# Modulation products of a transformer block: from two stationary columns and one accumulation to 32 stationary columns over four partition groups

## The chip, the cores and the metric

The program runs on one NeuronCore of one Trainium2 chip. The metric is the device time of one execution in microseconds (us). Before the change the median of three runs is 2926.92 us (2926.91 to 2927.85).

## What is computed

Two layers, one after the other, on 1024 tokens of width 1024. The part that the change touches is the modulation of the first layer: a conditioning vector `c` and a second one `c_ctx` go through silu and are multiplied with the 1024 x 6144 matrix `w_ada`; the six slices of the product shift, scale and gate the tokens.

```python
silu_c, silu_cc = silu(c), silu(c_ctx)[None]
mod_x = silu_c @ w_ada + b_ada                # 6 slices of 1024: sh1, sc1, g1, sh2, sc2, g2
mod_c = silu_cc @ w_ada + b_ada               # only the first two slices are used
hx = rms_norm(x, norm1_g) * (1 + sc1) + sh1   # needs slices 0 and 1
hc = rms_norm(ctx, norm1_g) * (1 + csc1) + csh1
qx, kx, vx, ux = split(hx @ w_in)             # keys and values of hc as well
attn = neighbourhood_attention(rope(qx), qx, rope(kx), vx, kc, vc, rpb)
conv = conformer_conv(ux, dw_kernel, ...)     # 31 taps
x = x + g1 * (concat(attn, conv) @ w_out)     # slice 2
x = x + g2 * squared_relu_mlp(rms_norm(x, norm2_g) * (1 + sc2) + sh2)   # slices 3, 4, 5
```

Behind it come the second layer (latent attention, a gated short convolution, attention over a memory) and a last norm, which the change leaves alone.

## The kernel before

Activations lie transposed: features on the 128 partitions, tokens in the free dimension. Weights come from memory in units of 128 x 1024 floats into `w_raw` (two buffers); GpSimd splits each into `w_hi` and `w_lo`, and TensorE makes each fp32 product of three faster products (L264 to L266). Each engine runs its own instruction list in the order in which the code writes it, and engines meet only on semaphores (`reach` waits for a count).

The first two slices of the modulation, 2048 columns, are made at the start, in four groups g of 512 columns (`ada_*`, L430 to L474). SP loads a group, 2048 KB, into one of two buffers; the loads of groups 2 and 3 wait until the products of groups 0 and 1 are done. TensorE takes silu of both vectors as the stationary operand, 2 columns for each of the 8 blocks of the contraction, and the group's columns as the moving one, and sums the 8 products in PSUM rows 0 and 1 (L449). ScalarE copies these two rows to `ada_row` (L464), TensorE turns them by four transposes so that the features come to lie on the partitions (L441), and VectorE adds the bias (L471 to L474). With that the first norm can be applied (`norm_act` L404, `norm_dve` L417 and L411), and with its first block the projections begin (L264).

The other four slices, 4096 columns, are made beside the neighbourhood attention (`late_*`, L488 to L521). The attention has 64 tiles (8 heads of 8 tiles of 128 queries). In step i TensorE makes the scores of tile i (L790 to L792), turns the probabilities of tile i-2 (L678), and makes the values of tile i-3 (L690). For odd tiles `late_pe` puts one late product in front of the values: the turn of the one before (L490) and then 8 products of 2 stationary columns with 128 moving ones (L500). Over the attention that is 32 late products, one for two tiles. Their weights use the two buffers of `w_raw`. VectorE in its step takes the row maximum with the bias (L742, L746), moves a part of the turned probabilities (L757), takes the late result (L505, L511) and scales the values (L765, L767), and then makes one or two taps of the convolution (L814). ScalarE takes the exponential (L711) and the other part of the move (L260). GpSimd makes the bias tables (L843).

One fp32 product, L449, L500, L678 or L690, may show as one or two records of TensorE in the profile: a transpose is one, an ordinary fp32 product is two.

The same code has `packed_sums` (L332 to L335): four products of 32 stationary columns each, into PSUM partitions 0, 32, 64 and 96. L910 in `ln_variance_pe` writes the same four groups, but four products in a row to the same group.

Of the kernel before, what the change touches and what calls it, by code (L numbers as in the profile page):

```python
# [23 lines left out]
ALU = mybir.AluOpType  # L24
ACT = mybir.ActivationFunctionType
AX = mybir.AxisListType.X

P = 128
T = 1024
TT = T // P  # L30
HALF = 512
D = 1024
KD = D // P
# [62 lines left out]
def build(nc, x_t, ctx_t, mem_t, w_ada, w_ada_late, units, small, rope_c, rope_s, rpb_pad, mask, positions, out, x_spill,  # L96
# [7 lines left out]
    def fixed(name, shape, offset, dt=F32):  # L104
        return nc.alloc_sbuf_tensor_at(name, [P, *shape], dt, offset=base + offset)

    def place(name, shape, kib, dt=F32):

        return nc.alloc_sbuf_tensor_at(name, [P, *shape], dt, offset=arena + int(kib * 1024))

    KIB = 1024
    w_raw = fixed("w_raw", [2, 1024], 0)
# [3 lines left out]
    ident = fixed("ident", [P], 40 * KIB)  # L116
    ones = fixed("ones", [P], 40 * KIB + 512)
    par = fixed("par", [N_SMALL], 41 * KIB)
    der = fixed("der", [N_DERIVED], 41 * KIB + (4 * N_SMALL + 31) // 32 * 32)
    assert 4 * N_SMALL + 32 + 4 * N_DERIVED <= 2 * KIB  # L120

    def sp_(name, n=1, k=0):
        return par[:, SMALL[name] + k:SMALL[name] + k + n]
# [1 line left out]

    mod_x, mod_c = der[:, 0:48], der[:, 48:64]
    a1, a1c, a2 = der[:, 64:72], der[:, 72:80], der[:, 80:88]
    silu_c = der[:, 88:104]
    qh_s, mq_s = der[:, 104:105], der[:, 105:106]
    one_col = der[:, 106:107]  # L130
    eps_col = der[:, 107:108]
    both_g = der[:, 128:136]
    row_max, neg_max, row_sum, inv_sum = (der[:, 112 + 4 * i:116 + 4 * i] for i in range(4))


    ada_buf = place("ada_buf", [2, KD, HALF], 0)
    ada_row = place("ada_row", [2, HALF], 32)
    ctx_sb = place("ctx_sb", [KD, CTX], 36)
# [23 lines left out]
    late_row = place("late_row", [P], 62)  # L162
# [47 lines left out]
    region = nc.alloc_psum_tensor("region", [P, 2, T], F32)  # L210
    aux = nc.alloc_psum_tensor("aux", [P, T], F32)
    pv = nc.alloc_psum_tensor("pv", [P, 2, HALF], F32)
# [5 lines left out]
    def sem(name):  # L218

        tag, _, what = name.partition("_")  # L220
        if tag in SHARED:
            name = f"{SHARED[tag][0]}_{what}"
        if name not in sems:
            sems[name] = nc.alloc_semaphore(name)
        return sems[name]

    def reach(e, name, value):

        tag, _, what = name.partition("_")
        if tag in SHARED:  # L230
            kind, before = SHARED[tag]
            value = value + sum(COUNTS.get(f"{t}_{what}", n) for t, n in before)
        e.wait_ge(sem(name), value)

    raw_loaded = [sem("raw_loaded_0"), sem("raw_loaded_1")]
    free = [sem("region_free_0"), sem("region_free_1")]
# [17 lines left out]
    def wait_region(e, use):  # L254

        if use >= 2:
            e.wait_ge(free[use % 2], use // 2)

    def copy(e, dst, src, **kw):
        return e.activation(dst, src, ACT.Copy, **kw)  # L260
# [169 lines left out]
    def ada_sp(e, pos):  # L430
        for g in range(N_ADA):
            if g >= 2:
                reach(e, "ada_mm", g - 1)
            e.dma_start(ada_buf[:, g % 2], w_ada[g]).then_inc(sem(f"ada_ld{g % 2}"), 16)

    def ada_pe(e, pos):
        def turn(g):
            reach(e, "ada_row", g + 1)
            for j in range(4):
                m = 4 * g + j  # L440
                last = e.transpose(pv[:, 0, 2 * m:2 * m + 2], ada_row[0:2, g % 2, j * P:(j + 1) * P], ident[0:2, 0:2])  # L441
            last.then_inc(sem("ada_tr"), 1)

        for g in range(N_ADA):
            use = pos.next_use()
            wait_region(e, use)
            reach(e, f"ada_ld{g % 2}", 16 * (g // 2 + 1))
            for k in range(KD):
                last = e.matmul(region[0:2, use % 2, 0:HALF], silu_c[:, 2 * k:2 * k + 2], ada_buf[:, g % 2, k],  # L449
                                start=(k == 0), stop=(k == KD - 1))  # L450
            last.then_inc(sem("ada_mm"), 1)
            if g:
                turn(g - 1)
        turn(N_ADA - 1)

    def ada_act(e, pos, ch):
        for g in range(N_ADA):
            use = pos.next_use()
            reach(e, "ada_mm", g + 1)
            if g >= 2:  # L460
                reach(e, "ada_tr", g - 1)
            copy(e, ada_row[0:2, g % 2], region[0:2, use % 2, 0:HALF]).then_inc(free[use % 2], 1)
            e.wait_ge(free[use % 2], use // 2 + 1)
            e.sem_inc(sem("ada_row"), 1)  # L464

# [10 lines left out]
    def constants_dve(e, ch):  # L476
        ch(e.memset(eps_col, EPS))
        e.sem_inc(sem("eps"), 1)
        reach(e, "small_ld", 16)
        ch(e.tensor_scalar(qh_s, sp_("qh"), QK ** -0.5, None, ALU.mult))  # L480
        ch(e.tensor_tensor(both_g, sp_("final", 8), sp_("norm_2", 8), ALU.mult))
        ch(e.tensor_scalar(mq_s, sp_("mq"), P ** -0.5, None, ALU.mult))
# [4 lines left out]
    N_LATE = 32  # L487

    def late_turn(e):
        return e.transpose(pv[:, 1, 256:258], late_row[0:2], ident[0:2, 0:2])  # L490

    def late_pe(e, i):
        if i % 2 == 0:
            return
        n = i // 2
        if n:
            late_turn(e)
        reach(e, f"late_ld{n % 2}", 16 * (n // 2 + 1))
        for k in range(KD):
            last = e.matmul(pv[0:2, 1, P:2 * P], silu_c[:, 2 * k:2 * k + 2], w_raw[:, n % 2, k * P:(k + 1) * P],  # L500
                            start=(k == 0), stop=(k == KD - 1))
        last.then_inc(sem("late_used"), 1)

    def late_add(e, ch, n):
        ch(e.tensor_tensor(mod_x[:, 16 + n:17 + n], pv[:, 1, 256:257], sp_("b_ada", 1, 16 + n), ALU.add))  # L505

    def late_dve(e, ch, i):
        if i % 2:
            if i > 1:
                late_add(e, ch, i // 2 - 1)  # L510
            ch(e.tensor_copy(late_row[0:2], pv[0:2, 1, P:2 * P]))  # L511

    def late_end_pe(e, pos):
        reach(e, "na_stored", HEADS * TT)
        late_turn(e).then_inc(sem("late_tr"), 1)
# [1094 lines left out]
    with nc.Block() as block:  # L1610
        @block.sync
        def _(sp):
            def load(u, s):
                sp.dma_start(w_raw[:, s], units[u]).then_inc(raw_loaded[s], 16)

            sp.dma_start(par[:], small).then_inc(sem("small_ld"), 16)
            ada_sp(sp, None)
            load(0, 0)
            load(1, 1)

            def load_range(a, b):
                with sp.Fori(a // 2, b // 2) as i:
                    for s in range(2):

                        sp.wait_ge(unit_split, i * 2 + (s - 1))
                        sp.dma_start(w_raw[:, s], units[i * 2 + s]).then_inc(raw_loaded[s], 16)

            load_range(2, ATTN_SPLIT)
            for s in range(2):
                sp.wait_ge(unit_split, ATTN_SPLIT - 1 + s)  # L1630
                sp.dma_start(w_raw[:, s], w_ada_late[s]).then_inc(sem(f"late_ld{s}"), 16)
            with sp.Fori(1, N_LATE // 2) as i:
                for s in range(2):

                    reach(sp, "late_used", i * 2 + (s - 1))
                    sp.dma_start(w_raw[:, s], w_ada_late[i * 2 + s]).then_inc(sem(f"late_ld{s}"), 16)
            reach(sp, "late_used", N_LATE)
            load_range(ATTN_SPLIT, N_UNITS)
            for j in range(KD):
                reach(sp, "out_ready", j + 1)  # L1640
                sp.dma_start(out[:, j], x3[:, j]).then_inc(sem("out_st"), 16)
            reach(sp, "out_st", 16 * KD)
# [42 lines left out]
        def _(act):  # L1685
            pos = Pos()
            ch = Chain(act, "scalar_step")
# [3 lines left out]
            act.dma_start(sin1[:], rope_s).then_inc(sem("rope1_ld"), 16)  # L1691
            act.dma_start(cos1[:], rope_c).then_inc(sem("rope1_ld"), 16)
            reach(act, "small_ld", 16)
            act.activation(silu_c, sp_("c", 16), ACT.Silu).then_inc(sem("silu_c"), 1)
            reach(act, "eps", 1)
            rms_act(act, ch, "r1", lambda k: x_sb[:, k], KD, T, D,
                    scale_from_ready=lambda k: reach(act, f"x_ld{k // 4}", 16))
            ada_act(act, pos, ch)
            reach(act, "ctx_ld", 16)
            norm_act(act, ch, "n1", KD, T, h_hi, lambda k: a1[:, k:k + 1], lambda k: mod_x[:, k:k + 1])  # L1700
# [59 lines left out]
        def _(dve):  # L1760
            pos = Pos()
            ch = Chain(dve, "vector_step")
            constants_dve(dve, ch)
            rms_dve(dve, ch, "r1", T)
            ada_dve(dve, pos, ch)
# [52 lines left out]
        def _(pe):  # L1818
# [11 lines left out]
            rms_pe(pe, "r1", KD, T)  # L1830
            reach(pe, "silu_c", 1)
            ada_pe(pe, pos)
            proj1_pe(pe, pos)
            tell()
# [194 lines left out]
```

## Time and profile before

| what | value |
|---|---|
| timed runs | 2926.92 us median of 3 |
| span of the profiled execution | 2924.9 us, 2.0 us under that median; the page gives no other time of that execution |
| TensorE busy | 2797.3 us, 96% |
| VectorE, ScalarE, GpSimd busy | 1366.1 us, 701.2 us, 937.5 us |
| modulation at the start (L449, L441) | 27.7 to 58.2 us |
| attention with the late products | 338.6 to 686.4 us |

The span runs from the first to the last instruction. The records of matmuls are pipelined: a record starts when its weights go in or its columns begin to stream, and the next may start before it ends.

### The profile page before, as it was taken

To read this page: it belongs to the slowest core of one execution; us is meant where nothing else is said; L and a number is where in the kernel's file an instruction comes from. 1 tells how busy PE (TensorE), PEld (TensorE's weight loads), DVE (VectorE), ACT (ScalarE), POOL (GpSimd) and SP (SyncE) were. 2 spreads that over 40 slices of the span, in tenths; PEclk is the share of its full clock that TensorE was granted. 3 is DMA by queue.
4 is the path that set the end of the run, shared out by engine and by line. 5 is a ranking of instruction groups with operands and counts; after the bars stand their busy time and mean duration, and the time that the engine had idled before them with its cause. 6 is when DMAs were issued, how large, how long until landed. Compare 5 with 4: busy or idle time off the path is not lost.

```text
span 2924.9 us, 34818 instructions
## 1 busy us (share of the span) xinstructions
PE 2797.3 (96%) x14040; PEld 2262.7 (77%) x14040; DVE 1366.1 (47%) x1493; ACT 701.2 (24%) x972; POOL 937.5 (32%) x443
## 2 busy tenths in 40 slices
PE   7999799998989999999988989999999999999899
PEld 2888577775868888888876769998888878878777
DVE  2735877774354454444457666663102231251331
ACT  3300133333131122121114445442100020141010
POOL 1334422110434353444432310002433434433333
PEclk9999799999989999999999999999999999999999
DMA  5111222112101111111111100000111111112112
GB/s 232 37 37 52 75 67 62 59 50 90 51 29 51 43 51 50 50 50 43 50 65 72 38 21 1 1 1 30 45 64 51 50 36 51 58 51 101 43 36 87
DMA packets 36673, 155.88 MB, mean 53 GB/s; under 512 B 4164, under 2 KB 4296, under 8 KB 35016
## 3 DMA queue, kind: packets, MB, share of 16 engines
q1 hardware_dynamic: 33264, 127.04, 13.0%
q10 hardware_dynamic: 1528, 20.71, 1.8%
q0 software_dynamic: 1760, 6.36, 0.9%
q8 instruction: 94, 1.54, 0.2%
q14 instruction: 27, 0.22, 0.0%
HBM read 145.70 MB, written 8.39 MB: 53 GB/s over the span
## 4 chain that ended last, share of the span: by engine, by line
PE 88%; DVE 8%; ACT 2%; DMA 1%; issue 1%; POOL 1%; DVEq 0%; ACTq 0%; POOLq 0%
PE region L264 21%; PE region L265 21%; PE region L266 21%; PE pv L690 8%; PE aux L678 4%; DVE conv L814 3%; PE region L790 2%; PE pv L500 2%; PE pv L341 1%; PE region L792 1%; PE aux L350 1%; PE region L449 1%; DVE tmp L417 1%; DVE h_lo L411 1%; DMA rs_again<-rs_spill 1%
## 5 line engine op out<-in xcount | busy, mean ns | idle before, releaser
L1649 POOL TENSOR_TENSOR w_hi<-w_raw,der 128x1024 fp32r<-128x1024 f32 x186 | 359.3, 1932 | 1713.5 <-PE region L266 1661.8
L264 PE MATMUL region<-h_hi,w_hi 128*128 128x512 f32 x1760 | 694.8, 395 | 40.8 <-DVE h_lo L411 17.8
L265 PE MATMUL region<-h_lo,w_hi 128*128 128x512 f32 x1760 | 690.6, 392 | 0.0
L266 PE MATMUL region<-h_hi,w_lo 128*128 128x512 f32 x1760 | 690.1, 392 | 0.0
L1652 POOL TENSOR_TENSOR w_lo<-w_raw,w_hi 128x1024 fp32r<-128x1024 f32 x186 | 497.2, 2673 | 14.6
L264 PEld LDWEIGHTS region<-h_hi,w_hi 128*128 128x128 f32 x1760 | 333.8, 190 | 119.9 <-issue 45.6
L266 PEld LDWEIGHTS region<-h_hi,w_lo 128*128 128x128 f32 x1760 | 333.8, 190 | 70.5
L265 PEld LDWEIGHTS region<-h_lo,w_hi 128*128 128x128 f32 x1760 | 334.0, 190 | 68.4
L264 PE MATMUL region<-ff_hi,w_hi 128*128 128x512 f32 x512 | 199.2, 389 | 0.0
L265 PE MATMUL region<-ff_lo,w_hi 128*128 128x512 f32 x512 | 199.2, 389 | 0.0
L266 PE MATMUL region<-ff_hi,w_lo 128*128 128x512 f32 x512 | 199.2, 389 | 0.0
L814 DVE SCALAR_TENSOR_TENSOR conv<-glu,par,conv 128x1024 f32<-128x1024 f32 x120 | 187.2, 1560 | 2.1
L1038 DVE TENSOR_TENSOR tmp<-tmp 128x1024 f32<-128x1024 f32 x32 | 63.8, 1995 | 184.5 <-ACT tmp L1010 184.5
L843 POOL TENSOR_TENSOR bias_t<-toep,mask_t 128x640 f32<-128x640 f32 x40 | 64.3, 1610 | 217.3 <-DVE der L746 217.2
L1052 DVE TENSOR_TENSOR tmp<-tmp 128x1024 f32<-128x1024 f32 x56 | 115.3, 2097 | 35.6 <-ACT tmp L1021 35.6
L690 PE MATMUL pv<-v,prob_t 128*128 128x128 f32 x1024 | 124.6, 275 | 0.0
L690 PEld LDWEIGHTS pv<-v,prob_t 128*128 128x128 f32 x1024 | 119.3, 192 | 0.0
L749 DVE TENSOR_REDUCE der<-region 128x1 f32<-128x1024 f32 (+1 forms) x96 | 91.5, 954 | 56.9 <-PE region L266 52.0
L1044 DVE SCALAR_TENSOR_TENSOR x<-region,der,x 128x1024 f32<-128x1024 f32 x32 | 41.1, 1283 | 152.7 <-PE region L266 152.7
L264 PEld LDWEIGHTS region<-ff_hi,w_hi 128*128 128x128 f32 x512 | 96.1, 188 | 20.0
L266 PEld LDWEIGHTS region<-ff_hi,w_lo 128*128 128x128 f32 x512 | 96.1, 188 | 19.9
L265 PEld LDWEIGHTS region<-ff_lo,w_hi 128*128 128x128 f32 x512 | 96.1, 188 | 19.9
(316 smaller groups left out, 4164.0 us busy)
## 6 DMA issues: line engine op xcount, KB each, us to landing
w_raw<-units SPq DMA_DIRECT2D x186, 512.0 KB, 3.6
w_raw<-w_ada_late SPq DMA_DIRECT2D x32, 512.0 KB, 3.7
ada_buf<-w_ada SPq DMA_DIRECT2D x4, 2048.0 KB, 11.9
toep<-rpb_pad POOLq DMA_DIRECT2D x16, 288.0 KB, 5.0
x_sb<-x_t ACTq DMA_DIRECT2D x2, 2048.0 KB, 13.6
x<-x_t ACTq DMA_DIRECT2D x1, 4096.0 KB, 14.3
x_spill<-x ACTq DMA_DIRECT2D x1, 4096.0 KB, 11.8
x<-x_spill ACTq DMA_DIRECT2D x1, 4096.0 KB, 14.4
```

The lines of the kernel that those rows point to most:

```text
L264: pe.matmul(dst, wh, xh, start=first, stop=False)
L265: pe.matmul(dst, wh, xl, start=False, stop=False)
L266: return pe.matmul(dst, wl, xh, start=False, stop=last)
L678: last = e.transpose(aux[:, b * P:(b + 1) * P], self.prob[:, i % 2, b * P:(b + 1) * P], ident[:])
L690: last = e.matmul(pv[:, i % 2, 0:P], self.prob_t[:, i % 2, b], self.v_of(i, b), start=(b == 0), stop=(b == self.nkt - 1))
L749: e.tensor_reduce(neg_max[:, i % 4:i % 4 + 1], region[:, use % 2, 0:self.nkeys], AX, ALU.max, negate=True).then_inc(self.s("maxed"), 1)
L814: ch(e.scalar_tensor_tensor(out=conv[:, j], in0=src, scalar=w, in1=conv[:, j], op0=ALU.mult, op1=ALU.add))
L843: e.tensor_tensor(bias_t[:, v, 0:KEYS].rearrange("p (r c) -> p r c", c=W_GRID), toep[h % 2][:, r0:r0 + 10], mask_t[:, v].rearrange("p (r c ...
L1038: e.tensor_tensor(tmp[:, 2 + f % 2], tmp[:, f % 2], tmp[:, f % 2], ALU.mult).then_inc(sem("ff_sq"), 1)
L1052: e.tensor_tensor(tmp[:, 2 + i], tmp[:, 2 + i], tmp[:, i], ALU.add).then_inc(sem("nf_acc"), 1)
L1649: pool.tensor_tensor(w_hi[:, s], w_raw[:, s], one_col.broadcast_to([P, 1024]), ALU.mult)\
L1652: pool.tensor_tensor(w_lo[:, s], w_raw[:, s], w_hi[:, s].bitcast(F32), ALU.subtract)\
```

## The change

The stationary operand of each block is widened from 2 to 32 columns (the two silu vectors repeated 16 times, `silu_wide`). Block k of the contraction goes to PSUM partitions 32 (k mod 4) to 32 (k mod 4) + 31, so that each group of partitions sums two blocks only. The four partial sums are added by the turn: instead of a transpose of two rows it is an ordinary fp32 product of the whole 128-row result with `quad`, 128 x 2, which has a one in column c for rows c, c+32, c+64 and c+96. The copies take 128 rows instead of 2. The semaphores `ada_mm` and `late_used` are raised by the last product of each group, so four times. VectorE makes `quad` once. To make room in SBUF, the scratch memory for DMA descriptors gets 8192 bytes a partition, which the program did not set before.

```diff
-            act.activation(silu_c, sp_("c", 16), ACT.Silu).then_inc(sem("silu_c"), 1)
+            act.activation(silu_wide[:].rearrange("p k (n two) -> p k n two", two=2),
+                           sp_("c", 16).rearrange("p (k two) -> p k two", two=2).unsqueeze(2).broadcast_to([P, KD, 16, 2]),
+                           ACT.Silu).then_inc(sem("silu_c"), 1)
...
             for j in range(4):
                 m = 4 * g + j
-                last = e.transpose(pv[:, 0, 2 * m:2 * m + 2], ada_row[0:2, g % 2, j * P:(j + 1) * P], ident[0:2, 0:2])
+                last = e.matmul(pv[:, 0, 2 * m:2 * m + 2], ada_row[:, g % 2, j * P:(j + 1) * P], quad, start=True, stop=True)
...
             for k in range(KD):
-                last = e.matmul(region[0:2, use % 2, 0:HALF], silu_c[:, 2 * k:2 * k + 2], ada_buf[:, g % 2, k],
-                                start=(k == 0), stop=(k == KD - 1))
-            last.then_inc(sem("ada_mm"), 1)
+                quarter = slice(32 * (k % 4), 32 * (k % 4) + 32)
+                last = e.matmul(region[quarter, use % 2, 0:HALF], silu_wide[:, k], ada_buf[:, g % 2, k], start=(k < 4), stop=(k >= 4))
+                if k >= 4:
+                    last.then_inc(sem("ada_mm"), 1)
...
-            copy(e, ada_row[0:2, g % 2], region[0:2, use % 2, 0:HALF]).then_inc(free[use % 2], 1)
+            copy(e, ada_row[:, g % 2], region[:, use % 2, 0:HALF]).then_inc(free[use % 2], 1)
...
+        reach(e, "consts", 4)
+        e.tensor_reduce(quad, ident[:].rearrange("p (q c) -> p c q", c=32)[:, 0:2], AX, ALU.add).then_inc(sem("quad"), 1)
...
-        return e.transpose(pv[:, 1, 256:258], late_row[0:2], ident[0:2, 0:2])
+        return e.matmul(pv[:, 1, 256:258], late_row[:], quad, start=True, stop=True)
...
         for k in range(KD):
-            last = e.matmul(pv[0:2, 1, P:2 * P], silu_c[:, 2 * k:2 * k + 2], w_raw[:, n % 2, k * P:(k + 1) * P],
-                            start=(k == 0), stop=(k == KD - 1))
-        last.then_inc(sem("late_used"), 1)
+            quarter = slice(32 * (k % 4), 32 * (k % 4) + 32)
+            last = e.matmul(pv[quarter, 1, P:2 * P], silu_wide[:, k], w_raw[:, n % 2, k * P:(k + 1) * P], start=(k < 4), stop=(k >= 4))
+            if k >= 4:
+                last.then_inc(sem("late_used"), 1)
...
-    nc = _bacc.Bacc("TRN2", target_bir_lowering=False, num_devices=1)
+    nc = _bacc.Bacc("TRN2", target_bir_lowering=False, num_devices=1, dynamic_dma_scratch_size=8192)
```

No instruction changes its place; what changes is what stands there. TensorE at the start, groups 0 to 2 of the early modulation, before (`region` is the PSUM tile, `der` held silu and `ident` the identity):

```order
L449 MATMUL region<-ada_buf,der 2x512 [waits ada_ld0,silu_c]
L449 MATMUL region<-ada_buf,der 2x512 x7
L449 MATMUL region<-ada_buf,der 2x512 [waits ada_ld1]
L449 MATMUL region<-ada_buf,der 2x512 x7
L441 MATMUL pv<-ident,ada_row 128x2 [waits ada_row]
L441 MATMUL pv<-ident,ada_row 128x2 x3
L449 MATMUL region<-ada_buf,der 2x512 [waits ada_ld0,region_free_0]
L449 MATMUL region<-ada_buf,der 2x512 x7
```

and the same place now (`der` here is `quad`):

```order
L452 MATMUL region<-ada_buf,silu_wide 32x512 [waits ada_ld0,silu_c]
L452 MATMUL region<-ada_buf,silu_wide 32x512 x7
L452 MATMUL region<-ada_buf,silu_wide 32x512 [waits ada_ld1]
L452 MATMUL region<-ada_buf,silu_wide 32x512 x7
L443 MATMUL pv<-der,ada_row 128x2 [waits quad,ada_row]
L443 MATMUL pv<-der,ada_row 128x2 x3
L452 MATMUL region<-ada_buf,silu_wide 32x512 [waits ada_ld0,region_free_0]
L452 MATMUL region<-ada_buf,silu_wide 32x512 x7
```

The products have 32 rows of output in place of 2, and the turn waits for `quad` too.

TensorE in the attention, one step with a late product, before:

```order
L792 MATMUL region<-k_ctx,q_t 128x256
L678 MATMUL aux<-ident,na_prob 128x128 [waits att_pt_b,att_pt_a,att_prob]
L678 MATMUL aux<-ident,na_prob 128x128 x6
L490 MATMUL pv<-ident,late_row 128x2 [waits att_stored,att_pt_b,att_pt_a]
L500 MATMUL pv<-w_raw,der 2x128 [waits late_ld1]
L500 MATMUL pv<-w_raw,der 2x128 x7
L690 MATMUL pv<-v_tok,na_prob_t 128x128 x5
L690 MATMUL pv<-v_ctx,na_prob_t 128x128 x2
```

and now (the lines have moved by five to six):

```order
L798 MATMUL region<-k_ctx,q_t 128x256
L684 MATMUL aux<-ident,na_prob 128x128 [waits att_pt_b,att_pt_a,att_prob]
L684 MATMUL aux<-ident,na_prob 128x128 x6
L495 MATMUL pv<-der,late_row 128x2 [waits att_stored,att_pt_b,att_pt_a]
L506 MATMUL pv<-w_raw,silu_wide 32x128 [waits late_ld1]
L506 MATMUL pv<-w_raw,silu_wide 32x128 x7
L696 MATMUL pv<-v_tok,na_prob_t 128x128 x5
L696 MATMUL pv<-v_ctx,na_prob_t 128x128 x2
```

The waits are the same, and the number of products is the same.

## Rows read from the trace of the kernel before

**Rows 1.** Page, part 4: the chain that ended last, by engine.

```profile
PE 88%; DVE 8%; ACT 2%; DMA 1%; issue 1%; POOL 1%; DVEq 0%; ACTq 0%; POOLq 0%
```

**Rows 2.** Chain of waits, 26 to 66 us: start us, us, what.

```profile
27.75 6.97 PE region L449 x16
...
34.74 7.85 DMA ada_buf<-w_ada
...
42.73 7.03 PE region L449 x16
...
50.09 6.97 PE region L449 x16
...
57.08 0.60 ACT ada_row L260
...
57.77 0.42 PE pv L441 x4
...
58.28 0.18 DVE der L471
```

**Rows 3.** Timeline at 420 to 434 us: start us, us, instruction, [idle before <- releaser].

```profile
421.72 1.92 DVE L814 SCALAR_TENSOR_TENSOR conv<-glu,par,conv 128x1024 f32<-128x1024 f32 x1
...
422.36 0.98 PE L678 MATMUL aux<-ident,na_prob 128*128 128x128 f32 x7
...
423.28 0.22 PE L490 MATMUL pv<-ident,late_row 2*128 2x2 f32 x1
...
423.43 1.91 PE L500 MATMUL pv<-w_raw,der 128*2 128x128 f32 x16
...
425.26 1.38 PE L690 MATMUL pv<-v_tok,na_prob_t 128*128 128x128 f32 x10
...
428.73 0.98 PE L678 MATMUL aux<-ident,na_prob 128*128 128x128 f32 x7
...
429.55 1.28 PE L690 MATMUL pv<-v_tok,na_prob_t 128*128 128x128 f32 x10
```

**Rows 4.** Timeline at 1532 us, the packed sums, two calls in a row.

```profile
1532.86 0.20 PEld L334 LDWEIGHTS aux<-tmp,ones 128*32 128x32 f32 x8 [7.09 <-DVE tmp L1052]
1532.87 1.94 PE L334 MATMUL aux<-tmp,ones 128*32 128x256 f32 x16 [6.67 <-DVE tmp L1052]
1533.30 0.20 PEld L334 LDWEIGHTS aux<-tmp,ones 128*32 128x32 f32 x4 [0.23 <-issue]
```

**Rows 5.** Timeline at 1642 us: packed sums, then unpacked products.

```profile
1642.01 0.64 PE L334 MATMUL aux<-tmp,ones 96*32 96x256 f32 x8
1642.58 1.99 PE L341 MATMUL pv<-head_scale,ident 128*128 128x256 f32 x8
```

**Rows 6.** Chain of waits over the whole span, at the layer norm.

```profile
709.36 5.71 PE aux L910 x28
```

**Rows 7.** Groups by line, 350 to 686 us: busy us, mean ns, idle before.

```profile
L814 DVE SCALAR_TENSOR_TENSOR conv<-glu,par,conv 128x1024 f32<-128x1024 f32 x75 | 108.7, 1449 | 0.6
...
L742 DVE CUSTOM_DVE_ANT_0 na_prob<-region,bias_t 128x896 f32<-128x896 f32 x62 | 67.7, 1091 | 26.4 <-PE aux L678 23.4 <-DVE conv L814 2.0
...
L500 PE MATMUL pv<-w_raw,der 128*2 128x128 f32 x512 | 61.1, 272 | 0.0
...
L505 DVE TENSOR_TENSOR der<-pv,par 128x1 f32<-128x1 f32 x31 | 4.9, 158 | 46.8 <-PE pv L690 46.8
```

**Rows 8.** Busy time by stretch: PE, PEld, DVE, ACT, POOL, clock, DMA share, GB/s.

```profile
4.00:8.00 4.00, 0.00 (x0) 0.00 (x0) 0.47 (x3) 0.91 (x2) 0.00 (x0) 1.00 1.02 429
64.00:68.00 4.00, 3.11 (x7) 2.48 (x8) 3.93 (x4) 3.60 (x4) 0.00 (x0) 0.50 0.00 0
```

**Rows 9.** Timeline of GpSimd at 51 us and of GpSimd and VectorE at 336 us.

```profile
51.00 1.89 POOL L1649 TENSOR_TENSOR w_hi<-w_raw,der 128x1024 fp32r<-128x1024 f32 x1 [49.34 <-DMA w_raw<-units]
...
336.34 2.29 POOL L843 TENSOR_TENSOR bias_t<-toep,mask_t 128x640 f32<-128x640 f32 x1
...
342.21 1.09 DVE L742 CUSTOM_DVE_ANT_0 na_prob<-region,bias_t 128x896 f32<-128x896 f32 x1 [3.71 <-PE region L792]
```

More of the change, by code:

```diff
@@ L127, in build @@
     a1, a1c, a2 = der[:, 64:72], der[:, 72:80], der[:, 80:88]
-    silu_c = der[:, 88:104]
     qh_s, mq_s = der[:, 104:105], der[:, 105:106]
@@ L132, in build @@
     both_g = der[:, 128:136]
+    quad = der[:, 136:138]
     row_max, neg_max, row_sum, inv_sum = (der[:, 112 + 4 * i:116 + 4 * i] for i in range(4))
+    silu_wide = place("silu_wide", [KD, 32], 164)
     ada_buf = place("ada_buf", [2, KD, HALF], 0)
@@ L432, in ada_sp @@
             if g >= 2:
-                reach(e, "ada_mm", g - 1)
+                reach(e, "ada_mm", 4 * (g - 1))
             e.dma_start(ada_buf[:, g % 2], w_ada[g]).then_inc(sem(f"ada_ld{g % 2}"), 16)
@@ L438, in turn @@
             reach(e, "ada_row", g + 1)
+            reach(e, "quad", 1)
             for j in range(4):
                 m = 4 * g + j
-                last = e.transpose(pv[:, 0, 2 * m:2 * m + 2], ada_row[0:2, g % 2, j * P:(j + 1) * P], ident[0:2, 0:2])
+                last = e.matmul(pv[:, 0, 2 * m:2 * m + 2], ada_row[:, g % 2, j * P:(j + 1) * P], quad, start=True, stop=True)
             last.then_inc(sem("ada_tr"), 1)
@@ L458, in ada_act @@
             use = pos.next_use()
-            reach(e, "ada_mm", g + 1)
+            reach(e, "ada_mm", 4 * (g + 1))
             if g >= 2:
                 reach(e, "ada_tr", g - 1)
-            copy(e, ada_row[0:2, g % 2], region[0:2, use % 2, 0:HALF]).then_inc(free[use % 2], 1)
+            copy(e, ada_row[:, g % 2], region[:, use % 2, 0:HALF]).then_inc(free[use % 2], 1)
             e.wait_ge(free[use % 2], use // 2 + 1)
@@ L510, in late_dve @@
                 late_add(e, ch, i // 2 - 1)
-            ch(e.tensor_copy(late_row[0:2], pv[0:2, 1, P:2 * P]))
+            ch(e.tensor_copy(late_row[:], pv[:, 1, P:2 * P]))
     def late_end_pe(e, pos):
@@ L1633, in _ @@
                 for s in range(2):
-                    reach(sp, "late_used", i * 2 + (s - 1))
+                    reach(sp, "late_used", i * 8 + 4 * (s - 1))
                     sp.dma_start(w_raw[:, s], w_ada_late[i * 2 + s]).then_inc(sem(f"late_ld{s}"), 16)
-            reach(sp, "late_used", N_LATE)
+            reach(sp, "late_used", 4 * N_LATE)
             load_range(ATTN_SPLIT, N_UNITS)
```

## The prediction

> **What bounds the kernel now.** I read the chain that ended last first: TensorE holds 88% of it [rows 1], so work taken from TensorE shortens the run wherever nothing else is close behind. Then the two places the change touches. At the start the chain goes through the 16 records of L449 of group 0, the load of group 2 that waited for them (7.85 us), the records of group 2 and of group 3, the copy, the turn, and the addition on VectorE at 58.28 [rows 2]. The reader is to see that the loads of groups 2 and 3 start only when the products of groups 0 and 1 are done, and that everything of layer one waits for 58.28. In the attention I read one step from the timeline: 0.22 us of turn (L490), then 16 records of L500 from 423.43, and the values (L690) at 425.26, with no idle time of TensorE [rows 3]. So the late product is on the path, 1.84 us of it with the drain behind it, 32 times. Last, the groups by line: VectorE still has idle time there, 46.8 us in front of L505 and 26.4 us in front of L742 [rows 7].
>
> **The late product.** Nothing here shows 32 stationary columns with 128 moving fp32 columns in four partition groups. The nearest row is the packed sums: 8 fp32 products in a row to groups 0, 1, 2, 3, 0, 1, 2, 3, which is the order of the new code. They show 16 records, and their weight loads lie in bunches, 8 at 1532.86 and the next 4 at 1533.30 [rows 4]: four products run at a time, and a wave of 256 columns takes 0.43 us there. The 16 records take 1.94 us in all; at 0.43 a record one after the other they would take 6.9. At the other clock level the same call of 8 records takes 0.64 us, against 1.99 us for 8 unpacked records of the same width [rows 5]. Taking the end of a record off (a 256-column record lasts 0.38 beyond the last start, as 1.99 less 7 spacings of 0.23), a wave costs 0.24 against 8 spacings of about 0.23.
>
> Before, 16 records of L500 take 1.84 us up to the next line, 0.109 us each ((1.91 - 0.27) / 15, with 0.272 for the length of one record [rows 3, 7]) and 0.09 of drain behind the last. After, they are four waves. The first needs its weights, 0.03 us; then three spacings of 0.109 and 0.02 for the stagger of four give the last start at 0.38; L690 comes 0.08 before the last record's end as before [rows 3], so with 0.27 - 0.08 behind it, L690 begins 0.57 us after the block's start. That is 1.27 us saved a time.
>
> The turn becomes an ordinary fp32 product with 128 rows, so two records of 128 weights each, 0.11 us apart as in L690 [rows 3], where a transpose was one. But L490 starts only 0.06 us before L678 ends, while L690 behind L678 in the step without a late product starts 0.16 us before it [rows 3]: the two-row transpose pays 0.09 for a change of the array's shape, and the 128-row turn doesn't. So +0.11 - 0.09, with a little less tail; I take it as -0.03, between -0.05 and +0.11 us a time. Sum in the attention: 32 x (1.27 + 0.03) = 41.6 us. Bounds: 32 x (1.27 - 0.11) = 37 and 43; the unpacked bound, no overlap at all, is a rival below.
>
> The Trainium skill, "TensorEngine Tiling (Array Packing)", Key Properties, says that changing the tiling mode drains TensorE. By that rule packing would add two drains to each late step; the trace agrees that such a change costs (the 0.09 above), but shows it on both sides of L500 before the change, since 2 columns are already handled as a narrow tile. The rule with nothing paid before would put the sum 32 x 0.18 = 6 us higher; the rows say zero.
>
> **What hides beside it.** The copies L511 and L464 take 128 rows instead of 2, but the same 128 or 512 elements a row; I take the same time. The wider silu writes 256 elements a row instead of 16 before the first square is due; `quad` is one small reduction on VectorE, some 25 us before it is needed. Both cost nothing while the loads of x last. The late loads of 512 KB have a period of 9.25 us instead of 10.55 and two buffers, so they stay hidden. Four increments instead of one reach only SP, which is not waited for.
>
> The Trainium skill, "TensorE: Matmul & The Clock Gate", The cost: per-tile semaphore tail, gives about 26 ns for each increment of packed products. No run here shows several. By its figure, an estimate, three more in each of 32 blocks would be 2.5 us if TensorE waited for them.
>
> **The start.** Groups 0 and 1 are ready in SBUF when TensorE comes to them at 27.7. Records of 512 columns follow each other every 0.43 us (6.97 / 16) [rows 2]. Four waves instead of 16 records: group 0's last product starts at 27.7 + 0.03 + 3 x 0.43 + 0.02 = 29.0 and ends at 29.6, and the load of group 2 goes out there instead of at 34.74. It lands 7.85 us later, at 37.5. The load of group 3 goes out at 31.4 behind it in the queue; 2 MB at the 429 GB/s that the DMA engines reach at the start [rows 8] are 4.9 us, so it lands at 42.4. Now the loads bind, and what is faster on TensorE is only the tail: four waves, copy 0.60, turn. TensorE has been idle from 32 to 37.5 and again before 42.4; between 58.2 and 64.9 before it fell to the lower clock, 0.50 of the granted clock [rows 8], so I take group 3 at 1.2 GHz: four waves of 0.85 and 0.35 of fill and tail, 3.8; copy 0.7 with its semaphores; 8 records of the turn at 0.17 (between 0.11 at the full clock and 0.22 at half) and its end, 1.6. VectorE's addition comes at 42.4 + 6.1 = 48.5 to 48.8 instead of 58.28. At 2.4 GHz it would be 2.2 us earlier. GpSimd's split of the first unit starts when it lands: before at 51.00 [rows 9]; its load now goes out right behind group 3 and lands 1 to 2 us after it, near 45, its first pass is 1.89 us, both I put at 4 to 5, so it is done by 50. The first projection came at 64.9 (3.11 us busy up to 68) [rows 8], 6.6 us behind the addition; it is due at 55.3 and finds the unit split. Saved: 9.5 us, between 6 (the loads run at 350 GB/s, or share more) and 12 (full clock).
>
> **Sum.** 41.6 + 9.5 = 51.1 us. The profiled execution's span of 2924.9 becomes 2873.8; the timed median lies 2.0 us over the span, which gives 2875.8, rounded 2876. With both terms at their bounds: 2872 to 2884. Everything behind the attention keeps its length, within some 3 us for where the clock's lower stretches fall.
>
> **Rivals.**
>
> *VectorE takes over the attention.* It has 73 us of idle time over 32 pairs of steps, 2.3 us each [rows 7]; TensorE gives up 1.3, so VectorE needs 8.25 of the new 9.25 us on average. But the taps are uneven: 75 in 31 pairs, so four pairs in ten have three; and a tap takes 1.45 us on average [rows 7] and 1.92 beside GpSimd [rows 3]. A pair with three taps at 1.92 needs 8.25 - 2.4 x 1.45 + 5.76 = 10.5. If VectorE's lag reached TensorE, 13 such pairs would cost 16 us at most; with half of the taps slow, 8: 2884. Against it: TensorE asks in step i for what VectorE began a step earlier, so a lag of up to 2 us is made up in the next pair. It decides when VectorE's lag passes 2 us.
>
> *The groups overlap only in part.* L910, which sends four products in a row to one partition group, takes 5.71 us for 28 records, 0.20 each, no better than unpacked [rows 6]: the order of the groups matters. If the two halves of each product had to follow in order, a block of 8 products would be 9 slots instead of 4: 1.1 us, 23 us saved in the attention and some 4 at the start, 2900. Against it: L334 has the new code's order and shows four waves [rows 4].
>
> *Slower: each change of partition group drains the array.* Rows 3 price a change of shape at 0.09 us. Were that paid at each of the 7 changes of group in a block, without overlap, a late product would take 1.84 + 0.63, and the turn's second record 0.11 more: +24 us in the attention, +2 at the start, 2953. It decides if one change of group costs more than what overlaps. Rows 4 and 5 speak against it. Its mild form is that the change does nothing: no overlap, no drain, 2931 with the turn.
>
> *The smaller descriptor memory holds GpSimd up.* Four loads go out before the first bias table at 336.34; VectorE then waits 3.7 us for TensorE at 342.21 anyway [rows 9]. If the loads had to wait for each other, some 14 us late, 10 would show: 2886. Later in the attention GpSimd has time enough.
>
> **Chances.** Forecast 75% (with the increments of the skill in it, 2878). VectorE 10%, partial overlap 7%, descriptor memory 4%, slower 2%, nothing gained 2%. The range of 2866 to 2888 holds the forecast, most of VectorE's case and the descriptor memory's; below the forecast it leaves room for a full clock at the start and a better placed clock later. A change of 0.2% (6 us) is what a measurement of this kernel can tell from none: faster by more 0.96, within it 0.01, slower 0.03.
>
> **What would show it.** In the profile after: the records of the late product in four bunches, about 0.64 us in all, and the values 0.57 us after its start; steps with a late product 1.3 us shorter, and the idle time of VectorE before L505's successor down from 1.5 us to a few tenths; the attention some 41 us shorter. At the start: groups 0 and 1 done by 31.4, two waits of TensorE for `ada_buf`, the addition near 48.6 and the first projection near 55. Wrong would be: TensorE waiting in the attention for L757 or L742's buffers; weight loads in the block one after the other; a load of group 3 landing after 46; or other stages that change by more than 3 us.

## The result and the profile after

The changed kernel takes 2876.95 us (median of 4 runs, 2874.46 to 2878.76) against 2926.93 before: ratio 0.9831, 95% interval 0.9817 to 0.9845. 2876 was predicted. Its profiled execution spans 2875.7 us, 49.2 less than before.

The attention, first the chip's view of one late step, the lines that answer to [rows 3] (timeline of TensorE at 407 to 409 us):

```profile
407.01 0.98 PE L684 MATMUL aux<-ident,na_prob 128*128 128x128 f32 x7
407.83 0.28 PE L495 MATMUL pv<-der,late_row 128*128 128x2 f32 x2
408.04 0.64 PE L506 MATMUL pv<-w_raw,silu_wide 128*32 128x128 f32 x16
408.62 0.60 PE L696 MATMUL pv<-v_tok,na_prob_t 128*128 128x128 f32 x3
```

The 16 records of the late product take 0.64 us instead of 1.91, and the values begin 0.58 us after the block's start instead of 1.83. The turn has two records now, but begins 0.16 us before L684 ends, not 0.06, and they start only 0.03 us apart: from the start of L684 to the start of the product 1.03 us pass, 1.07 before. The groups by line at 341 to 638 us (busy, mean ns, idle before) answer to [rows 7]:

```profile
L820 DVE SCALAR_TENSOR_TENSOR conv<-glu,par,conv 128x1024 f32<-128x1024 f32 x76 | 113.3, 1490 | 0.6
...
L748 DVE CUSTOM_DVE_ANT_0 na_prob<-region,bias_t 128x896 f32<-128x896 f32 x62 | 67.7, 1092 | 19.9 <-PE aux L684 17.1 <-DVE conv L820 1.1
...
L511 DVE TENSOR_TENSOR der<-pv,par 128x1 f32<-128x1 f32 x32 | 5.0, 156 | 11.9 <-PE pv L696 11.3 <-PE pv L495 0.5
```

In front of the last two VectorE waits 31.8 us instead of 73.2; nearly all of what TensorE gave up came out of VectorE's idle time.

The start, in the chain of waits at 26 to 57 us (start us, us, what), answering to [rows 2]:

```profile
28.64 3.69 PE region L452 x32
...
32.34 11.05 DMA ada_buf<-w_ada
...
43.53 1.92 PE region L452 x16
45.45 1.89 PE pv L443 x16
...
47.43 0.19 DVE der L474
...
47.85 1.24 DVE der L476
49.09 0.02 issue
49.11 1.83 DVE der L477
50.94 0.02 issue
50.96 4.52 DVE tmp L418 x2
```

Both first groups take 3.69 us where one took 6.97. Then the loads bind, as forecast. TensorE's granted clock was 0.56 of full when group 2 was multiplied and 1.00 for group 3 (busy time by stretch, columns as in [rows 8]):

```profile
38.00:42.00 4.00, 3.38 (x17) 0.79 (x17) 0.00 (x0) 0.00 (x0) 0.00 (x0) 0.56 1.03 442
43.00:48.00 5.00, 3.80 (x32) 2.36 (x32) 0.50 (x3) 0.60 (x1) 3.18 (x2) 1.00 0.41 164
```

What follows the addition is longer now, 9.3 us to the first projection instead of 6.6. GpSimd's splits of the first two weight units ran from 51.00 to 59.58 before, so that only the last of them met VectorE's work, which began at 58.28. These are the lines of before (timeline):

```profile
57.24 2.34 POOL L1652 TENSOR_TENSOR w_lo<-w_raw,w_hi 128x1024 fp32r<-128x1024 f32 x1
...
58.70 0.90 DVE L473 SCALAR_TENSOR_TENSOR der<-der,par 128x8 f32<-128x8 f32 x1
```

Now three of the four passes lie beside VectorE (timelines of GpSimd and of VectorE, answering to [rows 9]):

```profile
44.74 1.89 POOL L1655 TENSOR_TENSOR w_hi<-w_raw,der 128x1024 fp32r<-128x1024 f32 x1 [43.08 <-DMA w_raw<-units]
...
46.72 2.34 POOL L1658 TENSOR_TENSOR w_lo<-w_raw,w_hi 128x1024 fp32r<-128x1024 f32 x1
49.01 1.89 POOL L1655 TENSOR_TENSOR w_hi<-w_raw,der 128x1024 fp32r<-128x1024 f32 x1
50.98 3.41 POOL L1658 TENSOR_TENSOR w_lo<-w_raw,w_hi 128x1024 fp32r<-128x1024 f32 x1
```

```profile
47.43 0.17 DVE L474 TENSOR_TENSOR der<-pv,par 128x16 f32<-128x16 f32 x1 [10.98 <-PE pv L443]
...
47.85 1.22 DVE L476 SCALAR_TENSOR_TENSOR der<-der,par 128x8 f32<-128x8 f32 x1
49.11 1.82 DVE L477 SCALAR_TENSOR_TENSOR der<-der,par 128x8 f32<-128x8 f32 x1
50.96 4.52 DVE L418 TENSOR_TENSOR tmp<-x_sb,tmp 128x1024 f32<-128x1024 f32 x2
```

The two operations on 8 columns, L476 and L477, take 1.22 and 1.82 us and the two norm products (L418) 4.52, against 0.17, 0.17 and 2.36 when nothing runs on GpSimd (see units first below). Compare the ends: GpSimd's passes end at 49.06 and 50.91, and L476 and L477 end 0.02 us behind each; before, L473 ended 0.02 us behind GpSimd's 59.58. The other way round it looks the same: L418's first product began at 50.96, 0.02 us ahead of GpSimd's last pass, which then took 3.41 us instead of 2.34. So the one that starts later waits until the other is done; it is not that both run more slowly. The addition L474, which reads PSUM, took its 0.17 us in the middle of a pass.

Where the time went, from the start of the same instruction in each profiled execution (first projection, first score, first product of the layer norm's mean; the timed median is of each kernel's own runs):

| kernel | first projection | first score | layer norm | attention | span | timed median | ratio to before, 95% |
|---|---|---|---|---|---|---|---|
| before | 64.9 | 338.6 | 687.2 | 348.6 | 2924.9 | 2926.9 | |
| after | 56.8 | 331.9 | 638.4 | 306.5 | 2875.7 | 2877.0 | 0.9831 [0.9817, 0.9845] |
| late only | 64.9 | 338.5 | 646.2 | 307.6 | 2881.3 | 2884.2 | 0.9861 [0.9844, 0.9877] |
| start only | 55.9 | 329.7 | 678.3 | 348.6 | 2919.5 | 2921.5 | 0.9989 [0.9979, 0.9998] |
| groups in pairs | 57.9 | 332.8 | 640.0 | 307.1 | 2873.4 | 2878.1 | 0.9839 [0.9823, 0.9856] |
| wide, one group | 58.6 | 332.3 | 682.0 | 349.7 | 2922.9 | 2923.8 | 0.9993 [0.9983, 1.0003] |
| two groups | 56.4 | 330.2 | 671.9 | 341.6 | 2907.0 | 2910.0 | 0.9945 [0.9925, 0.9965] |
| eight increments | 56.0 | 329.8 | 637.0 | 307.2 | 2874.4 | 2875.8 | 0.9828 [0.9808, 0.9848] |
| descriptor memory only | 64.9 | 339.8 | 688.4 | 348.7 | 2923.4 | 2926.6 | 1.0001 [0.9991, 1.0010] |
| more on VectorE | 56.2 | 331.2 | 657.0 | 325.8 | 2891.9 | 2894.7 | 0.9897 [0.9882, 0.9913] |
| units first | 52.5 | 326.3 | 633.9 | 307.6 | 2869.0 | 2871.6 | 0.9818 [0.9805, 0.9832] |
| four buffers | 53.2 | 326.9 | 634.5 | 307.6 | 2869.6 | 2872.5 | 0.9818 [0.9805, 0.9832] |
| four buffers, units third | 52.8 | 326.5 | 633.9 | 307.4 | 2870.6 | 2872.5 | 0.9815 [0.9799, 0.9831] |
| four buffers, units fourth | 55.3 | 330.3 | 636.8 | 306.5 | 2873.5 | 2872.4 | 0.9814 [0.9800, 0.9827] |

The kernel before was run again beside each; its medians were 2925.6 to 2926.9, and the ratios are to the runs beside.

The first projection is a noisy number. Seven kernels of the table have the start of the change unaltered (after, start only, groups in pairs, wide, two groups, eight increments, more on VectorE), and it comes at 55.9 to 58.6 us. In five of them group 3 is multiplied at the full clock, in 1.9 us; in the other two, groups in pairs and wide, the clock had not risen or had fallen again, and the same records take 3.6 and 3.3 us. These two have the latest first projections, 57.9 and 58.6.

### The profile page after: what moved, and what is told of

It is laid out like the page before. It is cut to its first block, busy times and chain, and to the rows that moved or that the text cites. A ratio compares the mean times of both kernels' runs of the same rounds, so it can differ in the third digit from the quotient of the medians.

```text
span 2875.7 us, 34919 instructions
## 1 busy us (share of the span) xinstructions
PE 2737.6 (95%) x14088; PEld 2236.7 (78%) x14088; DVE 1374.4 (48%) x1494; ACT 701.9 (24%) x972; POOL 939.2 (33%) x443
## 4 chain that ended last, share of the span: by engine, by line
PE 87%; DVE 8%; DMA 1%; ACT 1%; issue 1%; POOL 1%; DVEq 0%; ACTq 0%; POOLq 0%; SPq 0%
PE region L265 22%; PE region L267 21%; PE region L266 21%; PE pv L696 8%; PE aux L684 4%; DVE conv L820 3%; PE region L796 2%; PE pv L342 1%; PE region L798 1%; DVE tmp L418 1%; PE aux L351 1%; PE pv L506 1%; DVE h_lo L412 1%; DMA rs_again<-rs_spill 1%; DVE x L1597 1%
## 5 line engine op out<-in xcount | busy, mean ns | idle before, releaser
L1058 DVE TENSOR_TENSOR tmp<-tmp 128x1024 f32<-128x1024 f32 x56 | 115.2, 2096 | 35.6 <-ACT tmp L1027 35.6
L1050 DVE SCALAR_TENSOR_TENSOR x<-region,der,x 128x1024 f32<-128x1024 f32 x32 | 41.1, 1284 | 152.7 <-PE region L267 152.7
```

Source lines behind the costliest of these rows:

```text
L1058: e.tensor_tensor(tmp[:, 2 + i], tmp[:, 2 + i], tmp[:, i], ALU.add).then_inc(sem("nf_acc"), 1)
```

## Experiments

**Late products only.** The early ones as before (2 columns, transposes).

```diff
-                last = e.matmul(region[quarter, use % 2, 0:HALF], silu_wide[:, k], ada_buf[:, g % 2, k], ...)
+                last = e.matmul(region[0:2, use % 2, 0:HALF], silu_wide[:, k, 0:2], ada_buf[:, g % 2, k], ...)
```

> Only the late products of the attention are packed; the early ones are as before (2 stationary columns, one group, transposed turn). Theory (each late step gives 1.3 us, 42 us over the attention, and the start gives the rest): 2926.9 - 42.5 = 2884.5 us, first projection at 65 us as before, attention 306.5 us long (348.6 before). Rival (the attention was shortened by something else, such as the smaller descriptor memory or the shift in time): over 2890, or a step that isn't 1.3 us shorter.

Measured 2884.19 us; first projection unchanged at 64.9, attention 307.6 us, 41.0 shorter. The late products alone carry five sixths of the gain.

**Start only.** The late products as before.

```diff
-            last = e.matmul(pv[quarter, 1, P:2 * P], silu_wide[:, k], w_raw[...], start=(k < 4), stop=(k >= 4))
+            last = e.matmul(pv[0:2, 1, P:2 * P], silu_wide[:, k, 0:2], w_raw[...], start=(k == 0), stop=(k == KD - 1))
```

> Only the early products are packed; the late ones are as before. Theory: the first projection comes at 56.8 us instead of 64.9, of these 8.1 us 1.4 are given back on VectorE before the attention, so 2926.9 - 6.7 = 2920.2 us. By the prediction's own term (9.5 us) it would be 2917.4. The two single parts should add up to the whole change (42.5 + 6.7 = 49.2, measured 50).

Measured 2921.54 us. The start gives 9.0 us at the first projection and all of it still at the layer norm (678.3), but the span is only 5.4 shorter. The loss is in the MLP. At three places in it, where a group of columns begins (995, 1171 and 1348 us), TensorE waits for nothing that the profile shows, in the first as follows (timeline):

```profile
993.11 0.39 PE L267 MATMUL region<-h_hi,w_lo 128*128 128x512 f32 x1
995.07 0.39 PE L265 MATMUL region<-h_hi,w_hi 128*128 128x512 f32 x1 [1.57 <-issue]
```

The three cost 5.9 us together against the kernel before, and TensorE's clock, at the lower level for 3.4 us from 1348.8, another 1.6. The wide, unpacked kernel below has the same three waits and one such stretch, 8.6 us in all; the changed kernel has none of them. In either run 3 to 4 us come back by 2725 us, which was not followed up. TensorE's instructions not being there in time would look like this, but no run here isolates it, and the cause stays open. So the parts, 41.4 and 4.1 us of timed median, don't add up to 50, though their pieces at the start and in the attention do.

**Groups in pairs.** Does the order of the partition groups make the overlap?

```diff
-        for k in range(KD):
+        for k in (0, 4, 1, 5, 2, 6, 3, 7):
```

> The change, with the late products in the order of partition groups 0, 0, 1, 1, 2, 2, 3, 3. Theory (the order of the groups makes the overlap, as in L910 before): the two halves and the two products of a group follow each other, neighbours overlap only at the seams: 13 slots of 0.109 us instead of 4, 1.55 us a block, 32 x 0.98 = 31 us more, 2908 us. With 9 slots it would be 2894. Rival (TensorE looks far enough ahead to mix the groups by itself): four waves, 2877.

Measured 2878.12 us, attention 307.1. The theory that the order 0, 0, 1, 1 spoils the overlap falls: the timeline shows four waves as before.

```profile
409.05 0.67 PE L506 MATMUL pv<-w_raw,silu_wide 128*32 128x128 f32 x16
409.64 1.38 PE L696 MATMUL pv<-v_tok,na_prob_t 128*128 128x128 f32 x10
```

**Two groups.** Four products in a row to one group, then four to the next. The turn takes 64 rows instead of 128.

```diff
-            quarter = slice(32 * (k % 4), 32 * (k % 4) + 32)
+            half = slice(32 * (k // 4), 32 * (k // 4) + 32)
```

> The change, with the late products in two partition groups only, blocks 0 to 3 in group 0 and 4 to 7 in group 1, four products (8 records) in a row each; the turn takes 64 rows. The run with the groups in pairs showed that TensorE mixes the groups by itself when 4 records of one group stand in a row. Theory (it looks only a few records ahead, and L910 before, with 8 records of a group in a row, hardly overlaps): a block takes 1.4 to 1.8 us, 27 to 39 us more than the change, 2904 to 2916. Rival (it looks over all 16 records): 8 waves, 1.0 us, 14 us more, 2891.

Measured 2910.01 us, attention 341.6 us. The values begin 1.46 us after the block's start:

```profile
423.83 0.38 PE L495 MATMUL pv<-der,late_row 64*128 64x2 f32 x2
424.14 1.53 PE L506 MATMUL pv<-w_raw,silu_wide 128*32 128x128 f32 x16
425.60 1.38 PE L696 MATMUL pv<-v_tok,na_prob_t 128*128 128x128 f32 x10
```

The starts of single records in this block are 424.14, .28, .39, .50, .60 for group 0, and the first of group 1 comes at 424.61, when 3 of group 0's 8 are still to start. (A record does not name its group; the spacing of 0.11 us within a group and the semaphore's increments tell them apart.) With 4 records to a group in a row all four groups started within 0.04 us. This would fit a limit on how many records of one group may wait, about three, before TensorE takes in no more. L910 before [rows 6] fits it too: its single records start one by one and then in pairs 0.006 to 0.03 us apart. The limit is inferred from these orders, not shown. The block accounts for 28 of the 35 us by which this attention is longer than the changed kernel's; most of the rest is the turn. From the start of L684 to the start of the product 1.22 us pass here and 1.03 there, 6 us over 32 steps: a turn of 64 rows costs 0.19 us more than one of 128.

**Wide, one group.** 32 stationary columns, all blocks in group 0, turned by the transpose.

```diff
-            last = e.matmul(pv[quarter, 1, P:2 * P], silu_wide[:, k], w_raw[...], start=(k < 4), stop=(k >= 4))
+            last = e.matmul(pv[0:32, 1, P:2 * P], silu_wide[:, k], w_raw[...], start=(k == 0), stop=(k == KD - 1))
```

> The start as in the change; the late products with 32 stationary columns, but all in partition group 0, and turned by the transpose as before. Theory (widening costs and gives nothing, packing is all): a block stays 1.84 us, 2920 us as with the start alone. Rival (weights of 32 columns are in the way): 0.025 us for each of 16 x 32 records, 13 us more, 2933. Rival (widening itself helps): under 2915.

Measured 2923.78 us. The block is 1.93 us long, as with 2 columns, and the attention 349.7:

```profile
417.37 0.22 PE L495 MATMUL pv<-ident,late_row 2*128 2x2 f32 x1
417.52 1.93 PE L505 MATMUL pv<-w_raw,silu_wide 128*32 128x128 f32 x16
```

Widening costs 1.1 us in 32 blocks and gives nothing; the overlap of the groups is all. Against the run of the start alone the span is 3.4 us longer: 2.7 of it stand at the first projection, with group 3 at the lower clock, and 1.1 in the attention. What both are slower than 2920 lies in the waits of the MLP named above and, here, in the start.

**Eight increments.**

```diff
-            if k >= 4:
-                last.then_inc(sem("late_used"), 1)
+            last.then_inc(sem("late_used"), 1)
```

> The change, with an increment of the semaphore behind each of the 8 late products instead of the last four. Theory (TensorE doesn't wait for them): the values begin 0.57 us after the block's start, 2877 us. Rival (the Trainium skill, TensorE: Matmul & The Clock Gate, The cost: per-tile semaphore tail, gives about 26 ns for each increment): 0.10 us more a block, 3 us over the attention, 2880.

Measured 2875.79 us. The values begin 0.57 us after the block's start, as with four increments, so TensorE doesn't wait for them:

```profile
406.56 0.65 PE L506 MATMUL pv<-w_raw,silu_wide 128*32 128x128 f32 x16
407.13 1.38 PE L695 MATMUL pv<-v_tok,na_prob_t 128*128 128x128 f32 x10
```

**Descriptor memory only.** The kernel before with `dynamic_dma_scratch_size=8192`.

> The kernel before, with the smaller memory for DMA descriptors alone. Theory (it costs nothing): 2926 us, GpSimd's four loads before the first bias table go out 0.6 to 0.9 us apart as before. Rival (the loads wait for each other): up to 10 us more, 2936.

Measured 2926.6 us, ratio 1.0001, 95% interval 0.9991 to 1.0010: no cost that can be measured.

**More on VectorE.** How far off is the next bound?

```diff
             ch(e.tensor_copy(late_row[:], pv[:, 1, P:2 * P]))
+            ch(e.tensor_reduce(spare[:], glu[:, 0, 0:T], AX, ALU.max))
```

> The change, with one reduction of 1024 columns more on VectorE in each of the 32 late steps (about 1.1 us; its result isn't used). VectorE has some 30 us of idle time left in the attention, 0.95 a pair. Theory (VectorE is now close behind TensorE): the 1.1 us use up the idle time and 0.2 to 0.5 us a pair show: 5 to 15 us more, 2882 to 2892. Rival (its lag is absorbed, TensorE is the only bound): within 2 us of 2877. Rival (VectorE is already the bound): 32 x 1.1 = 35 us more, 2912.

Measured 2894.65 us; attention 325.8 us, 19.3 longer. Groups by line of VectorE, and below them TensorE's wait in the same stretch:

```profile
L750 DVE CUSTOM_DVE_ANT_0 na_prob<-region,bias_t 128x896 f32<-128x896 f32 x62 | 67.7, 1091 | 4.6 <-PE aux L686 1.9 <-DVE conv L822 0.8
L519 DVE TENSOR_REDUCE spare<-glu 128x1 f32<-128x1024 f32 x32 | 39.0, 1220 | 1.1
```

```profile
PE aux L686 <- DVE na_prob_t L765: 14.1, 18, 1.2
```

The reduction takes 1.22 us, 39.0 in all. About half of it was absorbed. Of the 19.3 us that show, TensorE waits 14.1 for VectorE (L765); some 3 more are two stretches of 3.4 us at the lower clock, from 498.1 and from 607.3, which the changed kernel doesn't have there. The theory was right in kind and too small in size: VectorE still has about 22 us of idle time left in this attention, so not all of it can be used. Why not was not tested; I think that the waits of one step lie where the next one can't reach them.

**The start: units first.** The loads of the first two weight units ahead of groups 2 and 3.

```diff
         for g in range(N_ADA):
+            if g == 2:
+                load(0, 0)
+                load(1, 1)
             if g >= 2:
```

> The change, with the first two weight units loaded ahead of groups 2 and 3 of the early modulation. In the change GpSimd splits them from 44.7 to 54.4 us, beside VectorE's additions and first norm, and three of VectorE's instructions there take 1.2 to 2.3 us instead of 0.2 to 1.2. Theory (that overlap costs the 2.6 us between the addition and the first projection, 9.3 against 6.7 before): the split moves to 27 to 37 us, beside the reciprocal, the first projection comes 2.6 us earlier, at 54.2, 2874 us. Rival (the loads are moved into the way of group 3, nothing gained): groups 2 and 3 unchanged at best, 2877; if they take the queue up to 2.5 us longer, 2877 to 2879.

Measured 2871.63 us (2870.74 to 2875.01), first projection at 52.5. The timeline of GpSimd and of VectorE:

```profile
34.24 2.34 POOL L1659 TENSOR_TENSOR w_lo<-w_raw,w_hi 128x1024 fp32r<-128x1024 f32 x1
```

```profile
47.08 0.17 DVE L479 SCALAR_TENSOR_TENSOR der<-der,par 128x8 f32<-128x8 f32 x1
47.28 0.17 DVE L480 SCALAR_TENSOR_TENSOR der<-der,par 128x8 f32<-128x8 f32 x1
47.48 2.36 DVE L418 TENSOR_TENSOR tmp<-x_sb,tmp 128x1024 f32<-128x1024 f32 x2
```

With GpSimd done at 36.6, the operations on 8 columns take 0.17 us again and the pair of norm products 2.36. From the addition to the first projection 5.9 us pass, 9.3 in the changed kernel: the overlap with GpSimd cost 3.4 us. The kernel before, with 6.6, had paid 0.7 of this already. The theory had the size too small, 2.6 us, because it took 6.7 for the undisturbed stretch.

**Four buffers**, with no load waiting for a product, the units last, or third (between groups 1 and 2), or fourth (ahead of group 3). The last two add the lines of the run before, with `g == 2` and `g == 3`.

```diff
+    ada_more = place("ada_more", [2, KD, HALF], 96)
...
-            e.dma_start(ada_buf[:, g % 2], w_ada[g]).then_inc(sem(f"ada_ld{g % 2}"), 16)
+            e.dma_start((ada_buf if g < 2 else ada_more)[:, g % 2], w_ada[g]).then_inc(sem(f"ada_ld{g}"), 16)
```

> The change, with a buffer of its own for each group of the early modulation (groups 2 and 3 where the first norm's result comes later), so that no load waits for a product. Theory (in the change the start is bound by the two late loads: issued at 30.6 and 32.3, landed at 43.4): the loads follow each other from the start at 420 to 430 GB/s, group 3 lands at 37 to 38 us, the additions come 6 us earlier, 2871 us. Rival (the loads of x share the bandwidth and come later by what the new loads take): the sums of squares end later than 28.6, half of the gain or all of it goes, 2874 to 2878.

> Four buffers as above, with the two weight units loaded between groups 1 and 2. With four buffers TensorE ran group 3 and the last turns at the lower clock (6.5 us against 3.8 in the change), which took back most of what the earlier loads gave. Theory (the clock decides): groups 2 and 3 land earlier than in the change, but the additions come near 46 to 48 us, with VectorE undisturbed, 2870 to 2873 us as with the units first. Rival (the loads decide): additions at 44 us, 2868.

> As with four buffers, and the two weight units loaded ahead of group 3. Theory: the units' split leaves VectorE's way in part, group 3 lands 2.4 us later; the two cancel, 2870 to 2872 us. Rival (the split ahead of the additions is worth more than the 2.4 us): 2869 or less.

Measured 2872.54, 2872.49 and 2872.36 us. With the units last, group 3 lands at 38.02, 5.4 us earlier than in the changed kernel, as expected, but the addition comes at 44.71, only 2.7 us earlier. The timeline of TensorE shows why:

```profile
38.16 2.94 PE L451 MATMUL region<-ada_more,silu_wide 128*32 128x512 f32 x16 [2.61 <-DMA ada_more<-w_ada]
41.03 3.58 PE L442 MATMUL pv<-der,ada_row 128*128 128x2 f32 x16
```

The last 16 products and turns take 6.5 us at the lower clock, which holds from 38.9 to 59.4 us there, against 3.9 in the changed kernel, where it had risen at 41.5. With the units third the additions come at 46.89, undisturbed, though group 3 takes 3.6 us at the lower clock. None of the four orders of loads is clearly better than another: 2871.6 to 2872.5, 5 us under the changed kernel. The intervals of the ratios still overlap with the changed kernel's (0.9805 to 0.9832 against 0.9817 to 0.9845), so that the gain rests on the medians and on the first projection in the profiles together.

## Why the prediction was right, and where not

The forecast gain was 51.1 us, the spans show 49.2 and the timed medians 50.0.

- **The late product**, 32 x 1.30 = 41.6 us: measured 42.1 (306.5 against 348.6), and 1.29 to 1.30 from one pair of steps to the next throughout. The block's 0.57 us came out as worked, because a row with the same order, the same kind of product and the same four groups stood in the trace [rows 4]. The turn's -0.03 came out too, but not by its terms, which add up to +0.02 and left the rest to a guess: the two records start 0.03 us apart, not 0.11. From the first late product to the end of the attention 41.1 us were saved; 0.9 more lie between the first score and the first late product (20.6 us instead of 21.5), which isn't the late product's doing. Late products alone, without that, gave 41.0. The two drains a step, 6 us, that the prediction weighed and left out didn't come.
- **The start**, 9.5 us: measured 8.1 at the first projection, and 6.3 to 9.0 over the seven kernels with the same start. That it came near was partly luck, for three of its terms were off, in part against each other. The products began 0.9 us later in this execution. The loads took 12.8 us from the first issue (30.63) to the last landing (43.39), as estimated. Group 3 and the turn ran at the full clock, 3.9 us instead of 6.1, 2.2 better; in two of the seven kernels they ran at the lower one, as forecast. And "the first projection, 6.6 us behind the addition" failed: I followed the split of the first unit alone, which was done at 49.06, within the forecast, and asked only whether TensorE would find it. The second unit's split ran on to 54.4, both lay beside VectorE, and the stretch became 9.3 us. Loading the units first gives 3.4 us of it back.
- **What I let keep its length**: between the first projection and the first score the changed kernel takes 275.2 us instead of 273.7, the one of the start alone 273.8. The chain gives the last tap 2.61 us instead of 1.30, beside the first bias table:

```profile
327.95 2.61 DVE conv L820
```

```profile
327.94 1.52 POOL L849 TENSOR_TENSOR bias_t<-toep,mask_t 128x640 f32<-128x640 f32 x1
```

  The same 1.1 to 1.4 us appear with the descriptor memory alone and in three other runs (groups in pairs, more on VectorE, units fourth). In all five GpSimd's bias table begins ahead of VectorE's last tap, here by 0.01 us, and the tap takes 2.4 to 2.6 us; in the others the tap begins first and takes 1.29, and the bias table 2.1 to 2.6 instead of 1.5. So it is chance which of the two waits. Behind the attention 0.4 us were gained (49.2 - 48.8); at the memory attention the changed kernel stays at the lower clock for 6.8 us instead of 3.4 and loses 1.5, and gets it back elsewhere.
- **VectorE takes over** was rightly not the likeliest: no such wait cost time, but the distance is small. 1.22 us more a pair costs 0.6. The 2 us of lag that I thought made up in the next pair are not free: the run with more work shows TensorE waiting for L765 with much of VectorE's idle time unused.
- **Partial overlap**: the row I argued from, L910, was misread. Its 0.20 us a record are no sign of missing overlap: TensorE's clock was at the lower level from 709.1 to 712.5 us, where one record after the other would take 0.43 each, and the single records show pairs that start together. The order of the groups does matter, but only when it puts eight records of one group in a row (two groups); four in a row cost 0.02 us a block.
- **Slower**, and **nothing gained**, fell with the four waves: the changes of group cost nothing that shows (408.04 to 408.62), and one group gives nothing.
- **Smaller descriptor memory**: 1.0001. The increments: 0.57 us with four and with eight.

## What to carry to other kernels

A product with few stationary columns costs TensorE as much as a wide one (here 1.84 us for a block with 2 columns and 1.86 with 32); before packing it, look in the same trace for a packed product of the same kind, and take waves times the spacing of unpacked records. What a shortened stretch brings forward must be followed on every engine: here the weights' split moved beside VectorE's short operations and took 3.4 us of what the start had gained. When loads are moved earlier, ask at which clock TensorE will then work.

## What the runs showed of the hardware

- Four partition groups of 32 columns run at the full rate each: 16 fp32 records in four waves 0.11 us apart. The order 0, 0, 1, 1, 2, 2, 3, 3 is as good as 0, 1, 2, 3, 0, 1, 2, 3, while 0 four times and then 1 four times takes 1.46 us where eight waves would take 1.0.
- VectorE and GpSimd waited for each other whole here. Operations of VectorE on 8 columns, all operands in SBUF, that began while GpSimd's pass of 1024 columns was running ended 0.02 us behind it, whatever was left of it: 0.90 us before, 1.22 and 1.82 after, 1.67 with the groups in pairs, instead of 0.17. Additions on 16 columns with one operand in PSUM took 0.17 us beside the same passes. A pass that began 0.02 us behind VectorE's norm product took 3.41 us instead of 2.34.
- A fp32 turn of 128 rows with two moving columns, behind other 128-row products, takes no more of TensorE's time than a transpose of 2 rows: 1.03 us against 1.07 from the start of those products to the late one, and 1.22 with 64 rows. That it is the change of shape that costs is inferred from these three.
- TensorE's clock was at the lower level from 34.7 us, 2.5 us after its last product, and rose to the full level at 41.5, 3 us into group 2; with the loads ahead of it, and 2.6 us of waiting before group 3, it fell at 38.9 and stayed down for 20.5 us. With the same loads as in the changed kernel it stayed down for 27.3 us, from 35.6, in the run with the groups in pairs.
